# Hybrid NSA and S5 decoder block, one core: rotary embedding on head pairs with halves swapped by transfers, S and Y in four array quarters, compression layers side by side

## What is computed

```
h = rmsnorm(x); proj = h @ w_in            # q | kc vc | ksl vsl | kwi vwi | gl | gates | u | ...
qr  = rope(q);  ksl = rope(ksl);  kwi = rope(kwi)
rope(t): t1, t2 = halves of the 64 head channels
         [t1*cos - t2*sin,  t2*cos + t1*sin]
compress(kv): flat = blocks of 32 tokens (stride 16) + pos;  gelu(flat @ w1) @ w2      # for kc, vc
s5_scan(u): x[t] = A x[t-1] + B u[t] (complex, diagonal);  y = Re(C x) + D u
o_nsa = gates * (o_compressed, o_selected, o_window);  branch_a = (o_nsa * silu(gate)) @ w_proj_nsa
branch_b = (gelu(y) * sigmoid(gelu(y) @ w_glu + b) * silu(gate_s5)) @ w_proj_s5
out = rmsnorm(x + (sigmoid(mga)*branch_a + sigmoid(mgb)*branch_b) @ w_out)
```

## Time and profile before

| | us |
|---|---|
| three runs | 491.19, 494.63, 495.92 (median 494.63) |
| profiled execution, its own time | 491.93 |
| its span, first to last instruction | 490.1 |
| PE busy | 445.2 (91%) |
| DVE busy | 307.8 (63%) |
| ACT busy | 185.0 (38%) |
| POOL busy | 154.7 (32%) |

### The profile page before, as it was taken

The page is one execution under the profiler, slowest core; times in us unless marked ns, Lnnn a source line. Parts: engine busy times, 40 slices in busy tenths (PEclk is TensorE's granted clock), DMA queues, the critical chain, the costliest instruction groups (busy, mean ns, idle before and its releaser), DMA issues.

```text
span 490.1 us, 7307 instructions
## 1 busy us (share of the span) xinstructions
PE 445.2 (91%) x2811; PEld 359.4 (73%) x2811; DVE 307.8 (63%) x683; ACT 185.0 (38%) x371; POOL 154.7 (32%) x78
## 2 busy tenths in 40 slices
PE   0799999989969999979989989999999999999992
PEld 0588888779638896656656657888888888899991
DVE  1848899999999996997897883107124152072224
ACT  4552432242322245597546442223222322243323
POOL 0131454131022410233130332544454345344420
PEclk9879999999998999999999999999999999999997
DMA  9912631582473204801010100383333333233104
GB/s 244 294 45 73 186 86 43 63 164 81 139 211 85 44 1 92 239 16 44 1 43 2 45 27 17 86 305 101 111 86 93 107 102 86 94 104 105 44 0 171
DMA packets 68450, 47.53 MB, mean 97 GB/s; under 512 B 12760, under 2 KB 65440, under 8 KB 68256
## 3 DMA queue, kind: packets, MB, share of 16 engines
q1 hardware_dynamic: 66992, 46.70, 35.0%
q10 hardware_dynamic: 1424, 0.37, 0.5%
HBM read 42.87 MB, written 4.19 MB: 96 GB/s over the span
## 4 chain that ended last, share of the span: by engine, by line
PE 76%; DVE 10%; ACT 5%; DMA 3%; issue 3%; ACTq 1%; SPq 1%; DVEq 0%
PE bank L795 20%; PE bank L796 20%; PE bank L797 20%; PE bank L1018 3%; PE bank L1057 3%; PE bank L1036 3%; DMA raw<-in_w_in 2%; PE bank L936 2%; PE bank L907 1%; DVE prob L1457 1%; DVE z L1136 1%; DMA raw<-in_cmp_w_v 1%; DVE x_sb L1158 1%; ACT z L752 1%; DMA raw<-in_cmp_w_k 1%
## 5 line engine op out<-in xcount | busy, mean ns | idle before, releaser
L572 POOL TENSOR_TENSOR w_lo<-raw,w_hi 128x1024 fp32r<-128x1024 f32 (+2 forms) x57 | 138.1, 2423 | 281.7 <-ACT w_hi L609 281.7
L795 PE MATMUL bank<-hT_lo,w_hi 128*128 128x512 f32 x288 | 116.8, 406 | 0.0
L796 PE MATMUL bank<-hT_hi,w_lo 128*128 128x512 f32 x288 | 114.0, 396 | 0.0
L797 PE MATMUL bank<-hT_hi,w_hi 128*128 128x512 f32 x288 | 114.0, 396 | 0.0
L609 ACT ACTIVATE w_hi<-raw 128x1024 fp32r<-128x1024 f32 (+2 forms) x57 | 59.5, 1044 | 83.6 <-PE bank L797 68.3
L795 PEld LDWEIGHTS bank<-hT_lo,w_hi 128*128 128x128 f32 x288 | 55.6, 193 | 13.2 <-issue 1.8
L797 PEld LDWEIGHTS bank<-hT_hi,w_hi 128*128 128x128 f32 x288 | 55.2, 192 | 11.9
L796 PEld LDWEIGHTS bank<-hT_hi,w_lo 128*128 128x128 f32 x288 | 55.6, 193 | 11.0
L746 ACT ACTIVATE prob<-prob,nmax 128x128 f32<-128x128 f32 (+2 forms) x64 | 35.3, 552 | 25.6 <-DVE nmax L1457 25.6
L796 PE MATMUL bank<-w_hi,m_lo 128*128 128x256 f32 x128 | 36.2, 283 | 0.0
L797 PE MATMUL bank<-w_hi,m_hi 128*128 128x256 f32 x128 | 36.2, 283 | 0.0
(11 more groups left out here) (206 smaller groups left out, 753.0 us busy)
## 6 DMA issues: line engine op xcount, KB each, us to landing
raw<-in_w_in SPq DMA_DIRECT2D x32, 512.0 KB, 3.8
raw<-in_w_out SPq DMA_DIRECT2D x8, 512.0 KB, 3.4
x_sb<-in_x SPq DMA_DIRECT2D x4, 512.0 KB, 5.1
raw<-in_cmp_w_k SPq DMA_DIRECT2D x4, 512.0 KB, 3.8
raw<-in_cmp_w_v SPq DMA_DIRECT2D x4, 512.0 KB, 4.7
raw<-in_w_in SPq DMA_DIRECT2D x8, 256.0 KB, 3.8
raw<-in_w_proj_s SPq DMA_DIRECT2D x4, 512.0 KB, 3.4
raw<-in_w_proj_nsa SPq DMA_DIRECT2D x8, 256.0 KB, 3.8
```

Source lines behind the costliest of these rows:

```text
L572: nc.gpsimd.tensor_tensor(view(w_lo, j % NSPLIT, dims), w, view(w_hi, j % NSPLIT, dims).bitcast(F32), ALU.subtract).then_inc(lo_done, 1)
L795: nc.tensor.matmul(dst, w[0], x[1], start=first, stop=False, skip_group_check=True)
L796: nc.tensor.matmul(dst, w[1], x[0], start=False, stop=False, skip_group_check=True)
L797: return nc.tensor.matmul(dst, w[0], x[0], start=False, stop=last, skip_group_check=True)
```

## The change

- Rotary embedding. A q block is now one head of group 0 and the same head of group 1 (two transfers of 64 columns each), so that a bank is one full width `qn[:, t, :]`. ACT copies each of the six banks (q0 to q3, ksl, kwi) to SBUF in one instruction (`copy_out`). SP then copies the copy to a second tensor with the halves swapped, four transfers of 32 partitions x 512 (64 KB) for each bank (`swap_halves`). They stand in SP's list behind the loads named in `SWAP_BEHIND`: q0 behind q3, q1 behind ksl, q2 behind kwi, q3 behind kc, ksl behind vc, kwi behind val0. DVE waits for them (`swap_in`), and does bank x cos, swapped x sin, and the sum, each 128 x 512 (`rotate`). The sines are in PSUM bank 7, put there by ACT; the table pw is copied there once more afterwards.
- S and Y. Odd banks take their two halves crosswise (rows 0 to 63 of the array write partitions 64 to 127), and two banks are filled at once, so that four 64x64 quarters are addressed one after the other. ACT evacuates an odd S bank in two instructions of 64 partitions instead of one. Y goes to scratch in 16 transfers instead of 8.
- Compression. The first layers of k and v write two halves of one bank, H, matmul by matmul. Their weights are loaded between val0, val1, val2 and gs0 to gs2, and PE does val0, compress(0), val1, compress(1), val2, compress(2), gs0, compress(3), gs1, the transposes, gs2, the second layer, gs3. The second layer alternates the groups.

```
     b = [(f"u{t}", 1) for t in range(4)] + [(f"q{t}", 1) for t in range(4)]
-    b += [(n, 1) for n in ("ksl", "kwi", "kc", "vc", "val0", "val1", "val2")]
-    b += [(f"w1k{i}", 0) for i in range(4)] + [(f"w1v{i}", 0) for i in range(4)]
-    b += [(n, 1) for n in ("gs0", "gs1", "gs2", "gs3", "gn0", "gn1", "glu0", "gn2", "glu1", "gn3")]
+    b += [(n, 1) for n in ("ksl", "kwi", "kc", "vc")]
+    for i, n in enumerate(("val0", "val1", "val2", "gs0")):
+        b += [(n, 1), (f"w1k{i}", 0), (f"w1v{i}", 0)]
+    b += [(n, 1) for n in ( "gs1", "gs2", "gs3", "gn0", "gn1", "glu0", "gn2", "glu1", "gn3")]
...
+SWAP_BEHIND = ["q3", "ksl", "kwi", "kc", "vc", "val0"]
...
-        use(f"S{m}", (2, 4, 3)[m % 3])
+        use(f"S{m}", (2, 4, 3)[m % 3], 1 + m % 2)
...
-        use(f"Y{m}", 3 + m % 5)
+        use(f"Y{m}", (2, 4, 5, 6, 7)[m % 5])
...
+            def swap_halves(n, job, dst, src):
+                wait_copied(sp, job)
+                for at in range(4):
+                    to = 32 * (at ^ 1)
+                    sp.dma_start(dst[to:to + 32], src[32 * at:32 * at + 32]).then_inc(swap_in[n], 16)
...
+                if name in SWAP_BEHIND:
+                    n = SWAP_BEHIND.index(name)
+                    if n < HPG:
+                        swap_halves(n, f"q{n}", q_swap[:, n, :], qn[:, n, :])
+                    else:
+                        swap_halves(n, ("ksl", "kwi")[n - HPG], k_swap[:, n - HPG, :], kr[:, n - HPG, :])
                 if name == "q3":
                     u_to_scratch()
                 if name == "vc":
                     u_from_scratch()
...
+            def rotate(n, job, dst, swap, cos, done, count):
+                wait_copied(ve, job)
+                ve.wait_ge(swap_in[n], 64)
+                drain(V.tensor_tensor(dst, bk(job)[:, :], cos, MUL), job)
+                tt(sx_a[:, :], swap, sin_ps[:, :], MUL)
                 wait_drained(ve, job)
+                V.tensor_tensor(dst, dst, sx_a[:, :], ADD).then_inc(done, 1)
+                ve.wait_ge(done, count)
+
+            for r in range(HPG):
+                rotate(r, f"q{r}", qr[:, r, :], q_swap[:, r, :], rope[:, 0, :], qr_done, r + 1)
             for b, job in enumerate(("ksl", "kwi")):
+                rotate(HPG + b, job, kr[:, b, :], k_swap[:, b, :], rope[:, 1, :], kr_done, b + 1)
...
+                for kk in range(4):
+                    for r, (n, flat) in enumerate(pair):
+                        ins = nc.tensor.matmul(bk("H")[SN * r:SN * r + SN, 0:256], flat[:, 4 * i + kk].rearrange("p g n -> p (g n)"),
+                                               w1[n][:, kk, :], start=(i == 0 and kk == 0), stop=(i == 3 and kk == 3),
+                                               skip_group_check=True)
```

More of the change, by code:

```diff
@@ L155, in bank_plan @@
     for m in range(8):
-        use(f"S{m}", (2, 4, 3)[m % 3])
+        use(f"S{m}", (2, 4, 3)[m % 3], 1 + m % 2)
     for i, b in enumerate((2, 4, 3, 0)):
         use(f"V{i}", b, 2)
-    for n, b in (("HK", 1), ("HV", 2), ("HT", 4)):
-        use(n, b)
-    use("KCMP", 3, GROUPS)
+    use("H", 1, 2)
+    use("gs0", 2)
+    use("HT", 4)
+    use("gs1", 3)
+    use("gs2", 1)
+    use("KCMP", 4, GROUPS)
     use("VCMP", 0, 4)
[L163 to L166, removed]
+    use("gs3", 2)
+    for m, b in enumerate((3, 1)):
+        use(f"SCC{m}", b, 2)
     for m in range(8):
-        use(f"Y{m}", 3 + m % 5)
-    for g in range(GROUPS):
-        use(f"PET{g}", 3 + g)
+        use(f"Y{m}", (2, 4, 5, 6, 7)[m % 5])
+    for g, b in enumerate((3, 1)):
+        use(f"PET{g}", b)
     steps = attention_steps()
@@ L347, in build_program @@
             "z_split"))
+        swap_in, sin_set = [sem(f"halves{n}_swapped_in") for n in range(HPG + 2)], sem("sine_in_psum")
         qr_done, kr_done, gate_done, flat_zero, vz_done = (sem(n) for n in (
@@ L658, in _, with copy_out @@
                         .then_inc(w_first, 1)
+            def copy_out(job, dst, scale):
+                evacuate(job, dst, bk(job)[:, :], scale=scale)
+                after(job)
             for t in range(4):
[L661 to L667, removed]
+                copy_out(f"q{t}", qn[:, t, :], -0.125)
+                if t == 1:
+                    ac.wait_ge(w_built, 8)
+                    nc.scalar.activation(sin_ps[:, :], rope[:, 2, :], ACT.Copy).then_inc(sin_set, 1)
+            for b, job in enumerate(("ksl", "kwi")):
+                copy_out(job, kr[:, b, :], 1.0)
             for m in range(4):
@@ L694, in _ @@
                 evacuate("KCMP", kcT[rows, g, :], bk("KCMP")[rows, 0:NC])
[L695 to L699, removed]
+            gate_s5(2)
+            gate_s5(3)
             for m in range(2):
@@ L924, in _, with compress @@
                     ins.then_inc(part_used, 1)
[L926 to L931, removed]
+            def compress(i):
+                pair = (("k", flat_k), ("v", flat_v))
+                if i == 0:
+                    pe.wait_ge(flat_zero, 2)
+                    wait_drained(pe, "kc")
+                    wait_drained(pe, "vc")
+                    open_bank(pe, "H")
+                w1 = {}
+                for n, _ in pair:
                     k = block_at[f"w1{n}{i}"]
                     pe.wait_ge(raw_full[k % NRAW], raw_count[f"w1{n}{i}"])
[L934 to L943, removed]
+                    w1[n] = view(raw, k % NRAW, (4, 256))
+                for kk in range(4):
[3 more added lines that the diff above has]
+                                               skip_group_check=True)
+                        if kk == 3 and i < 3:
+                            ins.then_inc(part_used, 1)
+                        elif kk == 3 and r == 1:
+                            fill(ins, "H")
+            for n in range(3):
+                token_values(n)
+                compress(n)
+            channel_major("gs0", "gs0")
+            compress(3)
+            channel_major("gs1", "gs1")
+            wait_drained(pe, "H")
             open_bank(pe, "HT")
```

156 lines of the change are left out of this document (80 added, 76 removed).

## The result

| | before | after |
|---|---|---|
| median of the runs, us | 494.35 (four: 491.19 to 495.92) | 507.79 (four: 506.66 to 510.37) |
| ratio, 95% interval | | 1.0301 [1.0252, 1.0351] |
| profiled execution: own time, span | 491.93, 490.1 | 506.66, 504.9 |
| mean granted clock | 0.977 | 0.951 |

A forecast was written before the change was run, and what follows sets the result against it. PE and DVE, both full, were taken to meet at 186 us, the later end starting attention. 11.7 + 1.8 = +13.5 us on 491.93 gives 505.4, or 508.1 on the median; forecast 507, range 499 to 513.

The forecast's parts named there:

- The kwi swap lands at 105.2, the rotary part ends at 107.4: Rotary part: the last swap, queued behind U_sh and val0, makes DVE end at 107.4 instead of 94.39, +13.0 us.
- Rival 1: Rotary part: the small swap is not held up by bulk and lands at 102.1; 502.8 on the median; chance 0.09.
- pw 0.3, gate -2.0: DVE's chain behind the rotary part: second pw copy +0.3 us, gate instruction -2.0; scan ends at 186.4, `cm_done` at 197.0.
- S in quarters: nothing; the S copies start at 113, val0 on PE at 119: S: no gain from quarters; ACT's wait for val1's load delays the S copies, and val0 on PE by 6.5 us.
- SCC done at 175, 11 us of slack: Compression: PE's gains are spent in its ring, SCC ends as now, and DVE's delay hides it; priced at nothing.
- Rival 2: PE's ring of loads becomes the bound, with SCC later than 188: up to 4 us more, 509 to 513; chance 0.10.
- Y 11.2 to 5.6; the fifth bank waits for the exponentials: Y: quarters take 5.6 us instead of 11.2, with a wait for ACT; PET starts at 197.6, not 185.9, +11.7 us.
- Rival 4: Quarters run two by two: Y's last four banks take 5.6 us, 506 to 508; chance 0.76 together with the forecast.
- Y through scratch and glu0: +1.8: Behind Y: 16 issues instead of 8 delay glu0's load, for which ACT waits: +1.8 us (0 to +5).
- the sum of 13.5: Whole kernel: 11.7 us at PET's start plus 1.8 for glu0, on the profiled execution's 491.93: 505.4.

The follow-up runs named there:

- e1: The changed kernel with kwi's swap ahead of the U_sh transfers in SP's list instead of behind val0: 497.63 us, ratio 1.0093 to the kernel before.
- e2: The kernel before with the new rotary part alone, kwi's swap behind val0 as in the change: 510.27 us, ratio 1.0352.
- e3: The kernel before with the new rotary part alone, kwi's swap ahead of the U_sh transfers: 493.78 us, ratio 1.0019.
- e11: The changed kernel with kwi's swap issued by ACT on its own ring, right behind the copy of KR: 502.72 us, ratio 1.018.
- e8: The changed kernel, kwi's swap still late, with ACT's split of val1 moved behind its S copies: 507.13 us, ratio 1.0321.
- e10: e5 plus powers before the first rotation, build_e in four pieces, PET's second job in bank 4, four Y copies before the exponentials: 492.24 us, ratio 0.9974.
- e12: e3 with the powers before the first rotation and build_e in four pieces behind q1, q2, q3 and ksl: 493.88 us, ratio 0.9993.
- e6: e5 with the powers and all of build_e moved ahead of DVE's first rotation: 496.15 us, ratio 1.0089.
- e7: e3 with the powers and all of build_e moved ahead of DVE's first rotation: 498.43 us, ratio 1.0148.
- e5: e1 with ACT's split of val1 moved behind its S copies: 491.93 us, ratio 0.9997.

## Why the prediction was right

507 was forecast, 507.79 measured, by the mechanism that was named: the late kwi swap, DVE's chain behind it, PE waiting. That the number fits to 0.8 us is luck in part. Several terms are off by one to six microseconds and hide behind a wait or cancel. Point by point, in the prediction's own terms:

- *The kwi swap lands at 105.2, the rotary part ends at 107.4.* 104.96 (DVE goes on at 105.08) and 107.10. Shown as the cause by e1 against the change (1.009 against 1.030) and e2 against e3 (16.5 us). U_sh was issued at 92.43 for 92.25; the four issues took 2.42 us where I had 2.0, and the last transfer made that up. Rival 1 (not held up by the bulk, 102.1) fell: 5.85 us, not 3.1. The prediction holds it off by the order within one ring; e11 shows that it falls without that order, too (5.53 us on another ring). The idle time was 17.5 us for "some 18".
- *pw 0.3, gate -2.0.* Three copies of 128 columns in 1.09, 0.36 each; the gate 0.20 for 2.25. Missed: POOL's split of val1 now runs 111.92 to 113.92, and a pair of multiplications of 16 columns beside it took 2.03 us, its twin 0.38. That gave 1.65 back, and most of the scan's 187.7 against my 186.4, and of `cm_done`'s 198.2 against 197.0, is this.
- *S in quarters: nothing; the S copies start at 113, val0 on PE at 119.* 111.75 and 120.72. The start came out 1.25 us early, by the load of val1; what I left out is the clock. After the stop of 5.52 us each group of 32 records took 1.98, not 1.10, and the window shows 0.51.
- *SCC done at 175, 11 us of slack.* 181.42, and 6.5 us. This is the term that I mis-sized most, by 6.4 us, over half of its cover. 1.7 of them stand already when val0 starts on PE; for the rest the windows show the same thing as for S, a mean granted clock of 0.86 from 107 to 181 us, where the kernel before had 0.98 from 94 to 175. No run isolates it. The verdict stood since PE still had to wait; e8 shows that 2 us of it, given back, change nothing. Rival 2 would have needed 188.
- *Y 11.2 to 5.6; the fifth bank waits for the exponentials.* The wait was 1.65 us, the last four banks ran 194.41 to 197.3, at the high clock again (groups of eight 0.22 us apart), and ended 0.9 us before `cm_done`. PET at 198.27 for 197.6: +12.4 for +11.7. The forecast took it from Y, with the softmax over at 197.0 just ahead; in the run it was the softmax, over at 198.21, that PE waited for. The two ends lie so close that the sum hardly shows it. Rival 4 (two by two, no faster than halves) fell: the last four banks took 2.9 us, not 5.6.
- *Y through scratch and glu0: +1.8.* Near in size by luck, wrong in mechanism. The 16 issues took 7.48 us for 5.45, but the load of glu0 cost ACT 1.72 us, less than the 2.15 before. In its place stood two things that I hadn't listed: PET's second bank is that of the first scores, so PE waits 0.83 us for ACT's peT copy (200.19; PET to scores 1.92 us, before 1.03), and PE was busy 1.6 us longer over the same matmuls (284.0 us from PET on, 282.4 before). 0.9 and 1.6 make the 2.4 to within 0.1. The first was shown by e10, where that wait is gone; the second was only read from the windows. It goes with a granted clock of 0.98 in that stretch for 0.99, and such a difference need not be the change's: executions of the kernel before itself lie 4 us and more apart, with mean granted clocks from 0.98 down to 0.96.

So the sum of 13.5 (measured: 14.7 on the profiled execution's time) had its large term right in place and size, and was short by 0.7 us at PET and by 0.6 behind it.

## What to carry to other kernels

Place a small transfer that gates a long chain by what stands ahead of it in the issuer's list, not by its bytes: here 256 KB behind a wait and 1.4 MB (U_sh and val0) cost 2% of the time with the rest of the change and 16.5 us without it, and an edit of the list gave it back. Where two engines meet at one point, work taken from either is worth only the slack of the other (e8, e12), and work taken from an engine that waits for a late input anyway is worth nothing (e3), so try the edits in all combinations before judging one; and fill an engine's waits only with pieces shorter than each single wait, since what it holds while it is late (a bank) stops the engine that feeds it (e6, e7). On an engine that serves many, look for the instruction that waits for a load ahead of copies that don't (the split of val1): it cost 0.9% once the first bound was gone.

## What the hardware showed that I had not expected

- Transfers of 64 KB within SBUF landed in 2.0 us when they met nothing, and in 5.5 to 5.9 us, the last of the four, behind the U_sh transfers on the same ring or beside them on the other. Which of ring order and load did it is not parted by these runs; the small difference between the two rings speaks for load.
- A DVE instruction of 16 columns with two SBUF inputs was held for 1.65 us by a POOL subtraction that had begun 0.21 us before it, until that one ended (112.13 to 114.16, POOL's 111.92 to 113.92). The Trainium skill (SBUF — State Buffer, SBUF: two separate sides) says that the port pair that the two engines share is locked for a whole instruction, and that the later one is blocked; the trace agrees, and an operation that takes 0.19 us by itself waited as long as the POOL instruction had left.
- Quarters of 64 x 64, with the two row halves crosswise in two banks, doubled the rate of halves. In Y eight records start every 0.22 us, in halves four. In S 32 records took 1.10 us at the high clock, where 128 records in halves had taken 7.20, 1.8 for 32. An estimate from the rows says that all four run at once: the matmuls of the first compression layer, which use all 128 rows, take 5.39 us for 24 records of 256 columns, 0.88 ns a column, S in halves 0.44, Y in quarters 0.21. But each group of S was followed by 0.77 us of waiting for ACT, so that S took as long as before: 7.4 us of copies in e5 for 7.20.
